# Delta-rule inverse in a hybrid decoder step: diagonal 16x16 blocks by substitution on VectorE, with rows spread through scratch memory

## What is computed

```python
lower = eye(c) + where(strict, beta[..., :, None] * decay * kk, 0.0)
rhs = concatenate([beta[..., None] * v, (beta * exp(g))[..., None] * k], axis=-1)
sol = triangular_solve(lower, rhs, left_side=True, lower=True, unit_diagonal=True)
u0, w = sol[..., :dv], sol[..., dv:]
# then, chunk after chunk:
u = u0 - w @ st.T
o = exp(g)[:, None] * (q @ st.T) + qk @ u
st = gend * st + u.T @ kdec
```

## Time and profile before

| | |
|---|---|
| median of 3 runs | 1677.81 us (1675.85 to 1680.12) |
| span of the profiled execution | 1673.4 us |
| TensorE busy | 1622.7 us, 97% |
| VectorE busy | 862.9 us, 52% |
| ScalarE busy | 535.1 us, 32% |
| GpSimd busy | 507.4 us, 30% |
| mean granted TensorE clock | 0.999 |
| DMA moved | 163.17 MB, 33.4% of 16 engines' time |

### The profile page before, as it was taken

One profiled execution on the slowest core, in us unless ns is written; L12 is line 12 of the kernel. 1 busy time (PEld: TensorE's weight loads), 2 busy tenths in 40 slices (PEclk: granted clock), 3 DMA queues, 4 the chain that ended last, 5 costly groups with the idle time before them and its releaser, 6 DMA issues. The chain is left out here.

```text
span 1673.4 us, 26271 instructions
## 1 busy us (share of the span) xinstructions
PE 1622.7 (97%) x10707; PEld 1551.8 (93%) x10707; DVE 862.9 (52%) x1256; ACT 535.1 (32%) x918; POOL 507.4 (30%) x379
## 2 busy tenths in 40 slices
PE   5999999999999999999999999999999999999999
PEld 4989989999999999999889989999989999889976
DVE  4657653344444442790287772444668551895611
ACT  6322243222222222233334442311145222654200
POOL 1424415343343312811254551222212221103400
PEclk9999999999999999999999999999999999999999
DMA  4212155222222114542276353135210332534521
GB/s 156 53 26 51 34 155 134 71 70 70 70 71 70 52 51 130 160 119 63 88 196 191 108 175 108 46 120 164 58 38 27 103 100 60 153 123 152 149 79 58
DMA packets 189364, 163.17 MB, mean 98 GB/s; under 512 B 18380, under 2 KB 157055, under 8 KB 188726
## 3 DMA queue, kind: packets, MB, share of 16 engines
q1 hardware_dynamic: 189246, 161.51, 33.4%
HBM read 131.38 MB, written 30.22 MB: 97 GB/s over the span
## 5 line engine op out<-in xcount | busy, mean ns | idle before, releaser
L276 POOL TENSOR_TENSOR wL<-w_raw,wH 128x1024 fp32r<-128x1024 f32 (+1 forms) x112 | 241.5, 2156 | 802.9 <-ACT wH L269 802.7
L335 PE MATMUL ps<-hH,wH 128*128 128x344 f32 x1920 | 457.0, 340 | 12.4 <-PEq L196 3.6
L335 PE MATMUL ps<-hL,wH 128*128 128x344 f32 x1920 | 418.7, 320 | 0.0
L335 PE MATMUL ps<-hH,wL 128*128 128x344 f32 x1920 | 417.8, 320 | 0.0
L335 PEld LDWEIGHTS ps<-hH,wH 128*128 128x128 f32 x1920 | 314.5, 189 | 26.2 <-issue 10.1
L335 PEld LDWEIGHTS ps<-hL,wH 128*128 128x128 f32 x1920 | 325.9, 189 | 0.2
L335 PEld LDWEIGHTS ps<-hH,wL 128*128 128x128 f32 x1920 | 323.5, 188 | 0.0
L269 ACT ACTIVATE wH<-w_raw 128x1024 fp32r<-128x1024 f32 (+1 forms) x116 | 108.5, 935 | 116.3 <-PE ps L335 107.4
L2891 POOL TENSOR_SCALAR fa_logits<-fox_c_bc,token_scalars 128x128 f32<-128x128 f32 (+7 forms) x32 | 59.9, 1872 | 55.1 <-PE ps L2916 35.7
L1846 ACT ACTIVATE d_m<-ps 128x512 f32<-128x512 f32 x48 | 28.7, 598 | 134.8 <-PE ps L2028 134.8
L1235 DVE SCALAR_TENSOR_TENSOR m_th<-m_th,ps 128x1032 f32<-128x1032 f32 x24 | 29.5, 1228 | 61.7 <-PE ps L335 56.7
(11 more groups left out here) (576 smaller groups left out, 2773.6 us busy)
## 6 DMA issues: line engine op xcount, KB each, us to landing
w_raw<-in_w_in SPq DMA_DIRECT2D x80, 512.0 KB, 5.1
m_th<-gate_spill SPq DMA_DIRECT2D x28, 516.0 KB, 4.5
gate_spill<-d_gate SPq DMA_DIRECT2D x18, 516.0 KB, 3.0
fa_kv<-in_cache_fox_k SPq DMA_DIRECT2D x32, 256.0 KB, 3.0
fa_kv<-in_cache_fox_v SPq DMA_DIRECT2D x32, 256.0 KB, 3.5
w_raw<-in_w_branch SPq DMA_DIRECT2D x32, 256.0 KB, 2.8
gate_spill<-fa_gate SPq DMA_DIRECT2D x10, 516.0 KB
x_rows<-in_x_prompt SPq DMA_DIRECT2D x8, 512.0 KB, 6.5
```

The source lines that it names most:

```text
L276: pool.tensor_tensor(self.wL[:, t % 2, 0:nk], self.raw_at(t)[:, 0:nk], self.wH[:, t % 2, 0:nk].bitcast(F32), ALU.subtract).then_inc(self.w ...
L335: last = pe.matmul(self.ps[:, b + g, 0:cols], w[:, t % 2, k], x[:, k, g * cols:(g + 1) * cols], start=(k == 0 and n == 0), stop=(k == nk - ...
```

## The change

The diagonal blocks of 16x16 are no longer reached by levels 0 to 3 but solved by substitution on VectorE. When `NU` of a chunk is there, SyncE writes its eight diagonal 16x16 blocks (4 heads each) to scratch memory with eight DMAs, waits for them, and reads them back with one DMA that gives each of the 16 partitions of a block the whole block (`NB_`, 128 partitions of 4 KB). Each partition then solves for its own row of the inverse in 15 steps of two instructions (`solve`), and one multiplication with a block mask places the rows in `Y` (`spread`). `turn` now turns `Y` into `X` and stands in slot 3. TensorE keeps the levels 16, 32 and 64, in slots 6 to 11. The identity copies on GpSimd are gone, the masks are fewer, `KS` has one buffer, and `SQ` shares the space of `M1`. On VectorE the order of the chunk is written anew.

```diff
@@ -1683,15 +1694,19 @@
 
 
     nc = K.nc
-    LV = 6
+    LV = 3
     SLOTS = 16
+    NS = P // SB16
     LO, UP, NEGM, STR = masks.LO, masks.UP, masks.NEGM, masks.STR
     with ExitStack() as c:
         sb = lambda n_, s, d=F32: c.enter_context(nc.sbuf_tensor("d" + n_, s, d))
         one = lambda n_: sb(n_, [P, H, P])
         two = lambda n_: sb(n_, [P, 2, H, P])
-        X, Y, M1, U, STG, O, SQ = (one(n_) for n_ in ("_x", "_y", "_m1", "_u", "_st_decayed", "_o", "_osq"))
-        NU, QKT, QG, VB, KS, KD_ = (two(n_) for n_ in ("_nu", "_qkT", "_qgT", "_vb", "_k_state", "_kdec"))
+        X, Y, M1, U, STG, O, KS = (one(n_) for n_ in ("_x", "_y", "_m1", "_u", "_st_decayed", "_o", "_k_state"))
+        NU, QKT, QG, VB, KD_ = (two(n_) for n_ in ("_nu", "_qkT", "_qgT", "_vb", "_kdec"))
+        SQ = M1
+        NB_ = sb("_blocks", [P, H, SB16, SB16])
+        YC, YT, I16 = sb("_y_block", [P, H, SB16]), sb("_y_term", [P, H, SB16]), sb("_eye_block", [P, SB16])
         ST, DT, W = (one(n_) for n_ in ("_state", "_dT", "_w"))
         RN, GC = units.RN, units.GC
...
@@ -1748,13 +1763,32 @@
                     sp.wait_ge(*K.emptied(t))
                     sp.dma_start(K.d_gate[K.gate_of[t]], GATE[:, g % 2]).then_inc(spilled[g % 2], 16)
 
+                def blocks(ch):
+
+                    sp.wait_ge(S["nu"], ch + 1)
+                    if ch:
+                        sp.wait_ge(S["block_in"], 16 * ch)
+                    for b in range(NS):
+                        part = slice(b * SB16, (b + 1) * SB16)
+                        sp.dma_start(K.d_blocks[b].rearrange("h m i -> m h i"), NU[part, ch % 2, :, part]
+                                     ).then_inc(S["block_out"], 16)
+                    sp.wait_ge(S["block_out"], 16 * NS * (ch + 1))
+                    if ch:
+                        sp.wait_ge(S["solved"], ch)
+                    sp.dma_start(NB_[:].rearrange("p h m i -> p (h m i)"),
+                                 K.d_blocks.rearrange("b h m i -> b (h m i)").unsqueeze(1).broadcast_to(
+                                     [NS, SB16, H * SB16 * SB16])).then_inc(S["block_in"], 16)
+
                 K.loads(sp, t0 + 3)
+                blocks(0)
                 rows(1)
                 for ch in range(NCH):
                     spill(tile_of(ch, 0) - 1)
                     if ch + 2 < NCH:
                         rows(ch + 2)
                     K.loads(sp, tile_of(ch, 0) + 3)
+                    if ch + 1 < NCH:
+                        blocks(ch + 1)
                     spill(tile_of(ch, 0))
                     K.loads(sp, tile_of(ch, 8) + 3)
...
@@ -1767,13 +1801,6 @@
             @block.gpsimd
             def _(pool):
                 g = K.G(pool)
-
-                def identity(ch):
-
-                    if ch:
-                        pool.wait_ge(S["u"], ch)
-                    g.step(pool.tensor_copy(X[:], mb(K.ident[:])))
-                    pool.tensor_copy(Y[:], mb(K.ident[:])).then_inc(S["first"], 1)
 
                 def prepare_gram(ch):
...
@@ -1865,8 +1889,8 @@
                     for s in range(SLOTS):
                         if s in (0, 8):
                             gate(tile_of(ch, s) - 1)
-                        if s < 12 and s % 2 == 0:
-                            level(ch, s // 2 + 1)
+                        if 6 <= s < 12 and s % 2 == 0:
+                            level(ch, s // 2 - 2)
                         if s == 1 and ch + 1 < NCH:
                             prepare_gram(ch + 1)
@@ -1903,19 +1927,41 @@
                     dve.wait_ge(S["tok"], ch + 1)
                     dve.tensor_tensor(VB[:, ch % 2], B[7], bc(tokv(ch, 2)), ALU.mult).then_inc(S["vb"], 1)
 
-                def first(ch):
+                def solve(ch):
+
+                    dve.wait_ge(S["block_in"], 16 * (ch + 1))
+                    v.do(dve.tensor_copy(YC[:], I16[:].unsqueeze(1).broadcast_to([P, H, SB16])))
+                    for m in range(SB16 - 1):
+                        n = SB16 - 1 - m
+                        term = dve.tensor_tensor(YT[:, :, 0:n], NB_[:, :, m, m + 1:SB16],
+                                                 YC[:, :, m:m + 1].broadcast_to([P, H, n]), ALU.mult)
+                        if m == SB16 - 2:
+                            term.then_inc(S["solved"], 1)
+                            dve.wait_ge(S["solved"], ch + 1)
+                        else:
+                            v.do(term)
+                        v.do(dve.tensor_tensor(YC[:, :, m + 1:SB16], YC[:, :, m + 1:SB16], YT[:, :, 0:n], ALU.add))
+
+                def spread(ch):
+
+                    if ch:
+                        dve.wait_ge(S["u"], ch)
+                    part = lambda x: x.rearrange("p (b i) -> p b i", i=SB16)
+                    dve.tensor_tensor(Y[:].rearrange("p h (b i) -> p h b i", i=SB16),
+                                      YC[:].unsqueeze(2).broadcast_to([P, H, NS, SB16]),
+                                      part(masks.BLK[:]).unsqueeze(1).broadcast_to([P, H, NS, SB16]), ALU.mult
+                                      ).then_inc(S["upy"], 1)
+
+                def first_x(ch):
                     dve.wait_ge(S["turned"], ch + 1)
-                    dve.wait_ge(S["first"], ch + 1)
-                    dve.wait_ge(S["nu"], ch + 1)
-                    dve.copy_predicated(X[:], mb(LO[:, 0]), BM).then_inc(S["upx"], 1)
-                    dve.copy_predicated(Y[:], mb(UP[:, 0]), NU[:, ch % 2]).then_inc(S["upy"], 1)
+                    dve.tensor_copy(X[:], BM).then_inc(S["upx"], 1)
 
                 def level(ch, l):
                     dve.wait_ge(S["dxy"], ch * LV + l)
                     if l < LV:
-                        dve.copy_predicated(X[:], mb(LO[:, l]), BX).then_inc(S["upx"], 1)
+                        dve.copy_predicated(X[:], mb(LO[:, l - 1]), BX).then_inc(S["upx"], 1)
                     else:
-                        dve.copy_predicated(Y[:], mb(UP[:, l]), BY).then_inc(S["upy"], 1)
+                        dve.copy_predicated(Y[:], mb(UP[:, 0]), BY).then_inc(S["upy"], 1)
 
                 def turned_x(ch, l):
@@ -1959,32 +2005,30 @@
                 dve.wait_ge(S["zero"], 1)
                 prepare_gram(0)
                 prepare_rows(0)
...
-                first(0)
+                v.do(dve.tensor_reduce(I16[:], K.ident[:].rearrange("p (b i) -> p i b", i=SB16), AX.X, ALU.add))
+                solve(0)
+                spread(0)
                 for ch in range(NCH):
                     if ch:
                         square_sums(ch - 1)
+                        norm(ch - 1)
+                    first_x(ch)
+                    if ch + 1 < NCH:
+                        prepare_gram(ch + 1)
                     level(ch, 1)
-                    if ch:
-                        norm(ch - 1)
                     turned_x(ch, 2)
+                    if ch + 1 < NCH:
+                        prepare_rows(ch + 1)
                     level(ch, 2)
+                    decayed(ch)
                     turned_x(ch, 3)
+                    rest(ch)
                     level(ch, 3)
                     if ch + 1 < NCH:
-                        prepare_gram(ch + 1)
-                    turned_x(ch, 4)
-                    level(ch, 4)
-                    if ch + 1 < NCH:
-                        prepare_rows(ch + 1)
-                    turned_x(ch, 5)
-                    level(ch, 5)
-                    decayed(ch)
-                    turned_x(ch, 6)
-                    rest(ch)
-                    level(ch, 6)
+                        solve(ch + 1)
                     state(ch)
                     if ch + 1 < NCH:
-                        first(ch + 1)
+                        spread(ch + 1)
                 square_sums(NCH - 1)
                 norm(NCH - 1)
@@ -2015,11 +2059,11 @@
                     last.then_inc(S["tok"], 1)
 
                 def turn(ch):
-                    pe.wait_ge(S["nu"], ch + 1)
+                    pe.wait_ge(S["upy"], ch * (LV + 1) + 1)
                     if ch:
                         pe.wait_ge(S["m1e"], ch * LV)
                     for h in range(H):
-                        last = pe.transpose(BM[:, h], NU[:, ch % 2, h], K.ident[:])
+                        last = pe.transpose(BM[:, h], Y[:, h], K.ident[:])
                     last.then_inc(S["turned"], 1)
 
@@ -2099,15 +2143,15 @@
                         gram(0)
                     if k == 4:
                         rows(0)
-                    if k == 5:
-                        turn(0)
                 for ch in range(NCH):
                     for s in range(SLOTS):
-                        if s < 12:
+                        if s == 3:
+                            turn(ch)
+                        if 6 <= s < 12:
                             if s % 2 == 0:
-                                product(ch, s // 2 + 1)
+                                product(ch, s // 2 - 2)
                             else:
```

(33 more changed lines are left out.)

1 line of the change is left out of this document (removed).

## The result

| | before | after |
|---|---|---|
| median, 4 runs each on one chip | 1676.83 us (1675.47 to 1680.12) | 1698.63 us (1697.00 to 1700.99) |
| span of the profiled execution | 1673.4 us | 1696.9 us |
| mean granted clock | 0.999 | 0.979 |

The ratio is 1.0132, with a 95% interval of 1.0118 to 1.0145: slower by 22 us. The forecast was 1697.

The account below looks back on a forecast made before the run. TensorE, busy 97% of the span, was taken to bound the kernel. The terms -46 + 37 + 14 + 14 = +19 us on the 1673.4 us span gave 1692, with 4.4 to the median 1697 us; range 1646 to 1712.

Parts of the forecast that it names:

- TensorE's small work: Products, transposes and updates removed from TensorE's slots: 5.76 us less a chunk, 46 us less in eight chunks.
- `output` waits for `norm`: Slot 3, chunks 1 to 6: TensorE idles 6.2 us behind `turn` until VectorE's `norm` ends, 37 us in all.
- first `turn` waits: Chunk 0, slot 3: TensorE idles 7 to 17 us for the first solve's `Y`; 14 us taken.
- clock: TensorE's granted clock falls after each of seven waits, 2 us lost each, 14 us in all.
- Slot 0: First slot of a chunk: keeps its length without its product, since step k = 0 waits for ScalarE to empty the banks.
- GpSimd's burst: Six GpSimd instructions for the next chunk, from 2.1 us behind the chunk boundary to about 11 us behind it.
- the twelve: Small VectorE instructions between the sum and `norm`: begin 2.0 us behind the boundary, eight pass before GpSimd's last burst instruction.
- the lock: A small VectorE instruction ends only when the GpSimd instruction running beside it has ended: 0.90 us instead of 0.16.
- fully disturbed case: Chunk 0's solve with GpSimd's work falling on it throughout: `Y` there at 313 us, against 303 undisturbed.
- the landing: Chunk 0's diagonal blocks read back from memory: 5.1 us, like a 512 KB load, so the solve starts from about 295.
- Rival 2: Small VectorE instructions pass GpSimd freely, only the first chunk waits: -30 us, 1648 us; chance 0.20.
- Rival 3: Diagonal blocks come late through memory in 64-byte pieces, so `turn` waits as well: +49 us, milder +40, 1718; chance 0.12.

Follow-up runs that it names:

- half a solve: Changed kernel with the first 7 of the solve's 15 substitution steps left out, so its result is wrong: 1643.57 us, 0.9799 of the kernel before.
- hold of the burst: Changed kernel with GpSimd's burst for the next chunk waiting for `norm` of the chunk before, chunks 1 to 6: 1654.3 us, 0.9871 of the kernel before.
- both holds: Changed kernel, GpSimd's burst waiting for `norm` in chunks 1 to 6, its chunk 1 preparation for the first `spread`: 1648.12 us, 0.9821 of the kernel before.

## Why the prediction was right

| term of the sum | forecast, us | measured, us | from |
|---|---|---|---|
| TensorE's small work | -46 | about -49 | 42.8 in seven chunks by the markers; the first taken like them |
| `output` waits for `norm` | +37 | +36.8 | 6 waits of 6.1 |
| first `turn` waits | +14 | +18.8 | one wait |
| clock | +14 | about +15 | 12.5 in six chunks, 2.2 in the first |
| sum | +19 | about +22 | markers +22.3, span +23.5, runs +21.8 |

- **Small work.** 6.16 us a chunk where 5.76 stood. Slot 0 behaved as reckoned. Slot 8, which holds the same instructions in both kernels, took 3.83 us before and 3.61 in the run with half a solve; the 0.2 us lies in front of `update`, which begins 0.37 us after the slot's last bulk instruction before (448.97 to 449.34) and 0.16 there (476.09 to 476.25); the rest of the difference is hundredths in other slots. What `update` stood for before was not followed.
- **The wait for `norm`.** The chain was right in each link: the solve ends at the boundary (443.22 against 443.05), GpSimd's burst starts 2.06 us behind it (forecast 2.1), eight of the twelve pass before L277, `norm` is done 12.1 us behind the boundary, chunk 7 does not wait. A small part of the fit is luck: the prediction's own links, 2.1 + 6.7 + 2.4 to the end of the burst, three small ones (0.6) and `norm` (0.7), add up to 12.5 and not to the 12.0 it names. The burst ran 6.3 us from L1813 to L277 instead of 6.7, which made up for the slip. The earlier trace rows held for what they showed, and the hold of the burst and the half solve show that the lock is the cause.
- **The first chunk** is the term that was missized: 18.8 is above the upper bound of 17. The lock's share was right (9.9 us by experiment, 10 between the two cases of the forecast). Of the 4.8 us above the 14 that I took, 3 are my choice of a value below the fully disturbed case, which is what came. The step that failed is the landing: "The load of 512 KB takes 5.1 us", from the median of weight loads. The transfer of the blocks took 8.3 us from its issue to the first copy (289.90 to 298.21), 3.2 more; TensorE came 1.1 us later than reckoned (297.1), and so the wait went past the bound by 1.8. Some 1.3 us of the 8.3 are the 768 KB of rows, issued 0.7 us behind it.
- **The clock.** 2.1 us a wait, forecast 2. After a wait of 6.1 us TensorE works 2.7 to 5.9 us at half speed, 4.1 on average, where I had 3.4 with edges after 1.95 us. The price is not the same each time, though the six waits are: four chunks can be told apart by their markers; beyond 38.0 us and their wait they take 1.5, 1.5, 2.5 and 2.9 us, about half of their 2.9, 2.7, 5.0 and 5.9 us at half speed. The forecast had one price for all, and the mean fitted. For the first chunk I have only the half of its 4.5 us at half speed, 2.2. By the rule of the Trainium skill (TensorE: Matmul & The Clock Gate, HAM oscillation) the clock falls in every round: here it fell at all seven waits of the changed kernel. Behind the shorter waits of the two runs that move `output` it did not fall every time (see the last section).
- **Rival 2** had the right size for the case without the lock: forecast 1648, and 1648.12 with both holds. This is partly luck: late blocks, and behind them GpSimd's work that was not held, cost 8 us there (1648.1 against 1640.0) that it did not know.
- **Rival 3** did not come in the changed kernel; late blocks came once the burst was held, but by SyncE's queue and not by the size of the pieces, and TensorE's waits stayed under 2 us a chunk.

## What to carry to other kernels

In this kernel a chain of small VectorE instructions cost its own length (7.0 us for the solve) only while GpSimd was silent; beside GpSimd's 128x512 operations it took up to 16.9. Before moving work there, lay the two engines' timelines side by side at that place, and let GpSimd's burst wait for the end of the chain where it has slack: here two waits are worth 50 us of the 59. After each cure, look for the queue that it delays, SyncE's above all, and look again at who meets whom; and judge the place of a wait by all that stands behind it on the engine that is late.

## What was not expected

- A shorter wait did not cost less clock on average. With `output` in slot 5, waits of 3.3 us, the six chunks lie 261.9 - 228.1 = 33.8 us above the undisturbed ones, 20.0 of them waits: 13.8 for the rest, against 12.5 with waits of 6.1 us. But the six differ. Behind the first the transposes run at full clock, 0.65 us, and behind the third at half, 1.12:

```profile
360.45 0.65 PE L2099 MATMUL ps<-ident,d_o 128*128 128x128 f32 x4 [3.33 <-DVE d_o L1984]
445.19 1.12 PE L2099 MATMUL ps<-ident,d_o 128*128 128x128 f32 x4 [3.33 <-DVE d_o L1984]
```

  The granted clock stays at 1.00 after the first, falls for 3.4 us some 1 us after the second has ended, and is 0.50 for 5.7 to 6.0 us after each of the last four. The chunks take 41.6, 43.2 and then 44.2 to 44.3 us. One slot later, with waits of 2.6 us, a fall follows three of the six (chunks of 43.4 us) and none the other three (41.8). So the length of a wait alone does not say what the clock will cost.
- The lock also holds instructions with one input and a scalar: L1980 took 1.02 us instead of 0.17, and the integer L103 took 1.13.
- Eight issues of 4 KB took 3.6 us on SyncE in most chunks of the changed kernel, and 7.8 to 10.3 us with both holds, where 1.25 MB of loads had been issued just ahead.
- Slot 0, where TensorE waits 0.7 us for a bank that ScalarE empties, took in 0.9 us of TensorE's work without getting longer.
